# Rotary partner rows of q and k fetched by SBUF-to-SBUF copies instead of a permutation product

## The reference

```python
def partial_rotary(t, cos, sin):
    half = ROT_DIM // 2
    t1, t2, rest = t[..., :half], t[..., half:ROT_DIM], t[..., ROT_DIM:]
    return jnp.concatenate([t1 * cos - t2 * sin, t2 * cos + t1 * sin, rest], axis=-1)
...
qa = partial_rotary(qa.reshape(b, s, 2 * N_HEADS_DIFF, HEAD_DIM), cos, sin)
ka = partial_rotary(ka.reshape(b, s, 2 * N_HEADS_DIFF, HEAD_DIM), cos, sin)
```

## Time and profile before

| | |
|---|---|
| median of 3 runs | 2843.63 us |
| the profiled execution, its own time | 2845.07 us |
| its span | 2843.0 us |
| PE busy | 2715.9 us, 96% of the span |
| VectorE busy | 1593.8 us, 56% |
| ScalarE busy | 1149.2 us, 40% |
| GpSimd busy | 83.3 us, 3% |
| mean share of the DMA engines' time in the loading queue | 25.9% |
| granted TensorE clock, mean | 0.975 of full speed |

### The profile page before, as it was taken

One profiled execution on the slowest core, in us unless ns is written; L12 is line 12 of the kernel. 1 busy time (PEld: TensorE's weight loads), 2 busy tenths in 40 slices (PEclk: granted clock), 3 DMA queues, 4 the chain that ended last, 5 costly groups with the idle time before them and its releaser, 6 DMA issues.

```text
span 2843.0 us, 38347 instructions
## 1 busy us (share of the span) xinstructions
PE 2715.9 (96%) x12473; PEld 2136.2 (75%) x12473; DVE 1593.8 (56%) x2511; ACT 1149.2 (40%) x1848; POOL 83.3 (3%) x87
## 2 busy tenths in 40 slices
PE   6999899999699989999979999999999999999999
PEld 4776588888477658888857776888887887788887
DVE  5654565454575456545465555544447888554442
ACT  3443354342344335434255554322235666332222
POOL 4000100000200010000010000000000000000000
PEclk8999899999899989999989999999999999899999
DMA  3221233333112113333311111333332222133333
GB/s 90 60 54 52 59 89 96 96 96 89 53 53 60 45 59 89 96 96 96 90 51 45 45 44 52 96 96 96 96 96 75 60 59 60 50 98 96 96 96 96
DMA packets 417199, 214.81 MB, mean 76 GB/s; under 512 B 6747, under 2 KB 415942, under 8 KB 417094
## 3 DMA queue, kind: packets, MB, share of 16 engines
q1 hardware_dynamic: 416144, 212.89, 25.9%
q10 hardware_dynamic: 950, 0.58, 0.1%
HBM read 211.34 MB, written 2.10 MB: 75 GB/s over the span
## 4 chain that ended last, share of the span: by engine, by line
issue 49%; PE 44%; DVE 3%; POOL 2%; ACT 1%; DMA 0%; DVEq 0%; POOLq 0%; ACTq 0%; SPq 0%
PE acc L608 36%; PE sc L1022 2%; POOL yT L568 1%; PE sc L879 1%; PE sc L863 1%; PE po L892 1%; PE po L925 1%; PE aux L918 0%; PE tp L863 0%; PE po L1045 0%; PE tp L879 0%; DVE w_lo L1184 0%; PE po L1042 0%; PE sc L1011 0%; DVE xT L1302 0%
## 5 line engine op out<-in xcount | busy, mean ns | idle before, releaser
L608 PE MATMUL acc<-h_hi,w_hi 128*128 128x512 f32 x2048 | 841.6, 411 | 62.4 <-DVE h_lo L1117 46.0
L608 PE MATMUL acc<-h_hi,w_lo 128*128 128x512 f32 x2048 | 805.9, 394 | 0.0
L608 PE MATMUL acc<-h_lo,w_hi 128*128 128x512 f32 x2048 | 805.3, 393 | 0.0
L1714 ACT ACTIVATE w_hi<-w_raw 128x1024 fp32r<-128x1024 f32 x398 | 420.5, 1057 | 744.8 <-PE acc L608 741.9
L1184 DVE TENSOR_TENSOR w_lo<-w_raw,w_hi 128x1024 fp32r<-128x1024 f32 x398 | 486.1, 1222 | 84.4 <-ACT w_hi L1714 82.9
L608 PEld LDWEIGHTS acc<-h_hi,w_hi 128*128 128x128 f32 x2048 | 388.8, 190 | 172.8 <-DVE h_lo L1117 55.4
L608 PEld LDWEIGHTS acc<-h_hi,w_lo 128*128 128x128 f32 x2048 | 388.8, 190 | 85.2
L608 PEld LDWEIGHTS acc<-h_lo,w_hi 128*128 128x128 f32 x2048 | 390.1, 190 | 76.6 <-issue 5.6
L608 PE MATMUL acc<-mid_hi,w_hi 128*128 128x512 f32 x1120 | 440.7, 393 | 6.5 <-DVE w_lo L1184 3.3
L608 PE MATMUL acc<-mid_lo,w_hi 128*128 128x512 f32 x1120 | 439.7, 393 | 0.0
L608 PE MATMUL acc<-mid_hi,w_lo 128*128 128x512 f32 x1120 | 438.3, 391 | 0.0
(11 more groups left out here) (308 smaller groups left out, 2718.5 us busy)
## 6 DMA issues: line engine op xcount, KB each, us to landing
w_raw<-in_mlp_w_dram SPq DMA_DIRECT2D x128, 512.0 KB, 4.1
w_raw<-in_w_in_dram SPq DMA_DIRECT2D x48, 512.0 KB, 3.8
w_raw<-in_w_gate_dram SPq DMA_DIRECT2D x44, 512.0 KB, 3.7
w_raw<-in_w_up_dram SPq DMA_DIRECT2D x44, 512.0 KB, 3.7
w_raw<-in_w_down_dram SPq DMA_DIRECT2D x32, 512.0 KB, 4.1
w_raw<-in_hg_w_in_dram SPq DMA_DIRECT2D x32, 512.0 KB, 4.0
w_raw<-in_sb_w_qkv_dram SPq DMA_DIRECT2D x24, 512.0 KB, 3.7
w_raw<-in_w_out_dram SPq DMA_DIRECT2D x16, 512.0 KB, 4.1
```

The source lines that it names most:

```text
L608: mm = pe.matmul(bank[:], w[:, k], r[:, k], start=(k == 0 and i == 0), stop=(k == k_tiles - 1 and i == 2))
L1714: ACTV(w_hi[:, slot], w_raw[:, slot], ACT.Copy).then_inc(w_rounded, 1)
```

## The change

The permutation product, its matrix and its two places in `aux_uses` are gone. Instead the loading queue (SyncE) copies the partner rows from `raw` into `rsin`: per rotation four copies, each 8 partitions by 512 float32 (16 KB), one for each half of each of the two heads. Their completion semaphore is `partner_in` (64 per rotation). The rows of `rsin` that aren't copied keep whatever finite values they held, and the sine there is 0. The sign that was in `rotT` now sits in the frequencies: a negative frequency for the lower eight rows gives a negative sine and the same cosine. VectorE multiplies `rsin` by `sinT` in place.

In the queue the copies of pair p+1's q stand behind the load of that pair's fourth following unit, those of k behind the load after that. They wait for `evacuated` of their unit, and, except for the first of all, for `qk_ready` of the rotation before, since `rsin` is one tile.

```diff
-            if k == 6 and p + 1 < NDIFF:
-                uses.append(("rot_q", p + 1))
-            if k == 9 and p + 1 < NDIFF:
-                uses.append(("rot_k", p + 1))
...
+            def load_partner(l, p, i):
+
+                u = 3 * p + i
+                sp.wait_ge(evacuated[u % 2], l * (U_LAYER // 2) + u // 2 + 1)
+                if p or i:
+                    sp.sem_inc(load_turn, 1)
+                    sp.wait_ge(qk_ready, l * 2 * NDIFF + 2 * p + i)
+                sp.sem_inc(load_turn, 1)
+                for head in (0, HD):
+                    for a, b in ((0, ROT_HALF), (ROT_HALF, 0)):
+                        sp.dma_start(rsin[head + a:head + a + ROT_HALF], raw[head + b:head + b + ROT_HALF]).then_inc(partner_in, 16)
...
                         load(l * (U_LAYER // 2) + n // 2, n % 2, w_in_t, l * KD, KD, q_col + i * DIFF_W)
+                        if 1 <= p <= NDIFF and i < 2:
+                            load_partner(l, p - 1, i)
...
-            steps(nc.gpsimd.memset(rotT[:], 0.0))
...
-            heads = rotT[:].rearrange("p (b c) -> p b c", b=2)
...
-                        for slot, name, i in ((6, "rot_q", 0), (9, "rot_k", 1)):
-                            if k == slot and p + 1 < NDIFF:
-                                u = 3 * (p + 1) + i
-                                use_aux((name, p + 1))
-                                pe.wait_ge(evacuated[u % 2], half0 + u // 2 + 1)
-                                pe.matmul(aux[:], rotT[:], raw, start=True, stop=True).then_inc(aux_done, 1)
...
-                last = v.memset(by_head[:, :, :, d], float(inv_freq[d]))
+                v.memset(by_head[:, :, 0, d], -float(inv_freq[d]))
+                last = v.memset(by_head[:, :, 1, d], float(inv_freq[d]))
...
                 def rotate(p, i):
-                    a = AUX[(("rot_q", "rot_k")[i], p)]
-                    v.wait_ge(aux_done, A + a + 1)
-                    TT(rsin, aux[:], sinT[:], ALU.mult).then_inc(aux_free, 1)
+                    n = l * 2 * NDIFF + 2 * p + i + 1
+                    v.wait_ge(partner_in, 64 * n)
+                    v.sem_inc(partner_turn, 1)
+                    steps(TT(rsin, rsin, sinT[:], ALU.mult))
                     steps(TT(rcos, raw, cosT[:], ALU.mult))
                     steps.wait()
-                    v.wait_ge(aux_free, A + a + 1)
                     TT((qT, kT)[i][p % 2], rcos, rsin, ALU.add).then_inc(qk_ready, 1)
```

More of the change, by code:

```diff
@@ L133, in block2_norm @@
     return KD * (2 * LAYERS + i), KD * (4 * LAYERS + i), added_base(2 * LAYERS + i - 1)
-VEC_STEPS_LAYER = 93
+VEC_STEPS_LAYER = 101
 SB_STEPS = 40
@@ L195, in two_blocks @@
         ones = sb("ones", [P, S])
-        rotT = sb("rotT", [P, P])
         cosT = sb("cosT", [P, S])
@@ L327, in two_blocks @@
         qk_ready = sem("qk_ready")
+        partner_in = sem("partner_in")
+        partner_turn = sem("partner_turn")
         score_done = sem("score_done")
@@ L549, in _ @@
                                         pattern=[[2 * h, HD // h], [0, h]], channel_multiplier=-1).then_inc(pool_consts, 1)
-            pool.wait_ge(pool_consts, 8 + len(HALVES))
+            pool.wait_ge(pool_consts, 6 + len(HALVES))
             def split(half, slot, k):
```

## The result

| | before | after |
|---|---|---|
| median, measured side by side, 7 runs each | 2843.55 us | 2853.10 us |
| lowest to highest | 2841.71 to 2845.43 | 2851.21 to 2859.61 |
| ratio, 95% interval | | 1.0037 [1.0025, 1.0048] |
| the profiled execution, its own time / its span | 2845.07 / 2843.0 | 2851.21 / 2849.5 |
| PE busy | 2715.9 us | 2709.1 us |

The change makes the kernel slower, by 9.5 us or 0.37%. The forecast was 2837.3 us with a range up to 2842.5; both the size and the direction were wrong. PE is busy for 6.8 us less, where sixteen products at the prediction's 0.86 us would be 13.8, and the kernel still ends 6.5 us later.

A forecast was written before the change was run, and what follows sets the result against it. The later of PE's products and VectorE's list bounds each stage. Stage -1 gains 4.3 us, stage 0 nothing, stages 1 and 2 of both layers 2.0: 6.3 us in total, giving 2837.3 us, range 2834.0 to 2842.5.

The forecast's parts named there:

- the prediction's 0.86 us: PE's row of products: the cost of one removed permutation product, 1.72 us for two in each of stages 0 to 2.
- The two runners: Start of each stage's first scores: the later of PE's own products and VectorE's list up to the rotated k decides.
- scores at 119.06 + d: Stages 1 and 2: next first scores start then, against 122.62 before; gain 3.56 - d a stage, at most 1.72 us.
- d: Time from the end of k's evacuation to the fourth copy's landing: 0.30 + 1.14 + 1.60 = 3.04 us, between 1.4 and 5.2.
- Stage -1: The stage without attention, PE the only runner: removing both products gains 2.16 us, 4.3 us over two layers.
- Stage 0 at no cost: First attention stage, held by VectorE: k's copies hidden in 4.32 us of room before the rotation; gain and loss 0.
- A copy of 8 rows lies between: 0.38 each, 1.14: Loading queue: three further issues before the last copy, each priced between 0.3 (one row) and 0.47 us (big ones).
- I take 1.6: Issue to landing of a 16 KB copy: 1.6 us, extrapolated from large transfers to size zero; upper bound 3.5.
- 1.2 of the 1.72 us that PE saves is spent waiting for the copies: Stages 1 and 2: the rotated k comes late, leaving a gain of 0.5 us a stage.
- Copies slower than 3.2: Rival: slower copies mostly spend the gain, 2840.3 us at 3.8, no gain at 4.6; chance 0.36.
- The slower rival: The wait for copies exceeds what was removed, stage 0 losing too past 4.32; about 2858 us at 6.9; chance 0.08.
- The edits at nothing: Later weight loads behind the copies, memsets and selects at the start, and reading `rsin` from SBUF: no cost.

The follow-up runs named there:

- experiment 7: The changed kernel with copies for pair 0 alone and the permutation products back for pairs 1 to 3; 2840.16 us, ratio 0.9990 to the kernel before.
- Experiment 5: The changed kernel with one of k's four copies left, q's four kept, so the result is not the reference; 2836.95 us, ratio 0.9975 to the kernel before.
- experiment 4: The changed kernel with two of k's four copies issued by ScalarE's queue instead of SyncE's; 2837.52 us, ratio 0.9983 to the kernel before.
- Experiment 1: The changed kernel with eight idle products on PE ahead of the first scores of stages 1 to 3; 2840.55 us, ratio 0.9992 to the kernel before.
- experiment 2: The kernel before, without copies, with a product of k's rotation repeated on VectorE 4 times (stage 0) or 7 times (stages 1, 2); 2875.83 us, ratio 1.0106.
- experiments 3: The changed kernel with k's partner rows made by the product again and only q's copied; 2840.03 us, ratio 0.9991 to the kernel before.

## Why the prediction was wrong

- **What bounds the kernel: right.** The two runners, PE's row and VectorE's list, decide the stages as described. The formula "scores at 119.06 + d", a stage of 28.02 us longer by d - 3.56, fits every d that was measured: 28.84 for 4.38 (measured 28.84), 27.94 for 3.48 (27.93), 26.83 for 2.37 (26.83).
- **Stage -1: right.** 2.16 us was the sum; 2.27 in the trace, and experiment 7 shows it alone (3.75 us in two layers, against 4.3).
- **Stage 0 at no cost: wrong by a little.** The room of 4.32 was right, d was 4.96 in layer 0; the cost was 0.67 us there and 0.18 in layer 1 (29.80 us).
- **"A copy of 8 rows lies between: 0.38 each, 1.14": the term that was mis-sized.** The price was interpolated between an issue of one row and one of a large load, as if it grew with the rows. It was 0.685, above both ends of the bound, 0.3 and 0.47. Three of them are 2.06 us. Experiment 5 takes all three away and shortens d by 2.01; experiment 4 takes two away (1.37) and shortens it by 0.90.
- **"I take 1.6" for the landing: too low.** It was 2.09 to 2.13, VectorE's hand-over included. Taking the size out of large transfers gave a fixed part that no small one had shown. The Trainium skill, page "DMA: Bandwidth & Descriptors", section "Anatomy of one DMA — SWDGE (gpsimd) path", puts the fixed cost at about 2.0; these copies, from SyncE's queue, agree with it in size. The wake was 0.23 for 0.30. Together d was 4.38 instead of 3.04, and by the prediction's own formula, with the two values of stage 0, the change is then worth 4.54 - 4 x 0.82 - 0.67 - 0.18 = 0.4 us: nothing.
- **The step that was missing.** "1.2 of the 1.72 us that PE saves is spent waiting for the copies" took a wait of PE to cost its length. A wait of 2.0 to 2.4 us in a row of dense products also brings 1.6 us at half clock behind it, five times in the profile, 8.0 us. Experiment 1 removes it without touching the copies' lateness, experiment 2 brings it about without a copy. With 8.0 less 0.4 the sum is 7.6 us; the medians show 9.5 and the spans 6.5. The prediction put this term at nothing without a reason, although the trace of the kernel before has such a case, a wait of 2.33 us for VectorE with half clock behind it:

```profile
1476.88 0.80 PE L608 MATMUL acc<-h_hi,w_hi 128*128 128x512 f32 x1 [2.33 <-DVE w_lo L1184]
1477.48 0.63 PE L608 MATMUL acc<-h_lo,w_hi 128*128 128x512 f32 x1
1477.90 0.63 PE L608 MATMUL acc<-h_hi,w_lo 128*128 128x512 f32 x1
1478.33 0.63 PE L608 MATMUL acc<-h_hi,w_hi 128*128 128x512 f32 x1
```

The products start 0.43 us apart here, and 0.23 apart ahead of the wait.
- **The rivals.** "Copies slower than 3.2" was the case at hand, with a chance of 0.36, but its times ended at no change. The slower rival asked for a d of 5.4 from one mechanism, the landing (its own sum gives 5.3 us there; 5.7 needs 5.5). A d of 4.4 was enough with the clock. The upper end of the range took d to 4.3 although the bounds reached 5.2.
- **The rule against small transfers.** The Trainium skill, page "DMA: Bandwidth & Descriptors", section "Rules for kernel authors", says that those under 64 KB pay mostly overhead. The trace agrees: with one copy of 16 KB in place of four the stage is 2.0 us shorter, nearly the 2.06 of the three issues. No run joined the four into one, so what joining gives isn't shown.
- **The edits at nothing: right.** q's copies, the later loads of weights and the start of the program cost nothing that shows (experiments 3 and 7).

Still open: what decides in which execution the stretches outside the starts appear, and why the start at 93.53 kept its clock after 2.42 us. A kernel with the copies joined into two was not tried.

## What to carry to other kernels

Price a small DMA on a path by its issues as well as its landing, and bound an issue by a row of its own kind, not between two others. When an edit takes work off a dense TensorE row but makes its input later, ask how long TensorE will stand, and look in the trace for a stop of that length and the clock behind it: here a stop of about 2 us cost nearly as much again in clock, and moving 0.7 us of products ahead of the waiting ones, with the copies split over two queues, turned a loss of 0.37% into a gain of 0.36%. Idle products that speed a kernel up are a quick test for this.

## What the hardware showed unexpectedly

- An issue of a 16 KB copy of 8 rows between places of SBUF takes 625 ns in SyncE's queue, one after another 0.685 us apart, more than the 425 ns of a 512 KB load in the same queue.
- Such a copy lands 2.09 to 2.13 us after its issue begins, alone or as the fourth.
- Ahead of the first scores of stages 1 to 3, TensorE's clock was at 1.2 GHz after stops of 1.63 to 3.15 us, not at every one, and never after stops of up to 0.97 us; after about 3 us the 7 us that follow ran at a mean of 0.53 to 0.56, after 1.6 to 2.3 us at 0.76. Elsewhere it also fell after two stops of 0.91 and 1.20 us close together.
- Two issues on ScalarE's queue kept its own next instruction back enough for PE to wait 0.58 us.
